# Input projection and causal pooling made one stage, with a late normalisation and the trunk stored in two halves

## What is computed

```python
h  = RMSNorm(x);  z = h @ w_in           # columns: q 512 | k/v cmp 256 | slc 256 | win 256 | gates 24 | u 512
# rope on the first 16 dims of each q and k head; sigmoid on the gates
# pooling, 4 groups of 128 channels of u, windows w = 2, 4, 8, 16:
win_sum = cs[:, t + 1, c0:c1] - cs[:, lo, c0:c1]
d = (win_sum / cnt - u32[:, T - n_out:, c0:c1]).astype(u_ext.dtype)
outs.append(d @ w_pool[g])
return jnp.concatenate(outs, axis=-1) * pool_scale
```

## Time and profile before

| | us |
|---|---|
| three runs, median (lowest to highest) | 3171.54 (3168.58 to 3177.47) |
| the profiled execution, its own time | 3173.93 |
| its span, first to last instruction | 3172.3 |
| PE busy in the span | 2825.5 (89%) |
| DVE busy | 1457.5 (46%) |
| ACT busy | 904.5 (29%) |
| POOL (GpSimd) busy | 338.6 (11%) |
| mean granted TensorE clock | 0.944 of full |

### The profile page before, as it was taken

How to read it: one execution, slowest core, us unless ns; L and a number is a source line. 1 busy time by engine, 2 the same in 40 slices (tenths; PEclk the granted TensorE clock), 3 DMA queues, 4 the chain that set the end, 5 groups by cost and what they waited for, 6 DMA issues and landing times. The chain is left out here.

```text
span 3172.3 us, 46324 instructions
## 1 busy us (share of the span) xinstructions
PE 2825.5 (89%) x17798; PEld 2592.6 (82%) x17798; DVE 1457.5 (46%) x2742; ACT 904.5 (29%) x1536; POOL 338.6 (11%) x342
## 2 busy tenths in 40 slices
PE   4999989999999998788478888677799999999997
PEld 4888879999999997788366666233789999999996
DVE  4444447445444444301437677221345444444545
ACT  4655642111111111211236556233141111111102
POOL 3444420000000000100012131211000000000000
PEclk9999999999999999899559989789899999999999
DMA  4213133112111101101200010663321111111101
GB/s 163 103 68 113 57 103 110 51 40 63 43 40 40 40 27 73 34 30 50 76 23 32 30 51 31 211 191 108 108 67 52 55 40 40 40 53 40 45 8 55
DMA packets 171244, 206.30 MB, mean 65 GB/s; under 512 B 11879, under 2 KB 155176, under 8 KB 168367
## 3 DMA queue, kind: packets, MB, share of 16 engines
q1 hardware_dynamic: 164311, 154.27, 15.9%
q0 software_dynamic: 6816, 50.49, 4.4%
HBM read 190.89 MB, written 18.01 MB: 66 GB/s over the span
## 5 line engine op out<-in xcount | busy, mean ns | idle before, releaser
L407 ACT ACTIVATE f_act_gate<-f_act_gate 128x352 f32<-128x352 f32 x132 | 65.8, 498 | 1186.1 <-DVE f_act_gate L464 1186.0
L501 DVE SCALAR_TENSOR_TENSOR trunk<-f_down,trunk 128x352 f32<-128x352 f32 x528 | 275.9, 524 | 207.7 <-PE f_down L104 207.7
L102 PE MATMUL f_up<-f_h_hi,f_gu_hi 128*128 128x352 f32 x1056 | 344.9, 327 | 0.0
L102 PE MATMUL f_gate<-f_h_hi,f_gu_hi 128*128 128x352 f32 x1056 | 344.6, 326 | 0.0
L104 PE MATMUL f_up<-f_h_hi,f_gu_lo 128*128 128x352 f32 x1056 | 343.2, 325 | 0.0
L104 PE MATMUL f_gate<-f_h_hi,f_gu_lo 128*128 128x352 f32 x1056 | 343.0, 325 | 0.0
L102 PE MATMUL f_down<-f_a_hi,f_wd_hi 128*128 128x352 f32 x1056 | 341.0, 323 | 0.0
L103 PE MATMUL f_gate<-f_h_lo,f_gu_hi 128*128 128x352 f32 x1056 | 340.9, 323 | 0.0
L103 PE MATMUL f_up<-f_h_lo,f_gu_hi 128*128 128x352 f32 x1056 | 340.6, 323 | 0.0
L103 PE MATMUL f_down<-f_a_lo,f_wd_hi 128*128 128x352 f32 x1056 | 338.8, 321 | 0.0
L104 PE MATMUL f_down<-f_a_hi,f_wd_lo 128*128 128x352 f32 x1056 | 338.4, 320 | 0.0
(11 more groups left out here) (338 smaller groups left out, 5594.7 us busy)
## 6 DMA issues: line engine op xcount, KB each, us to landing
as_pages<-in_cache_kv_slc_dram SPq DMA_DIRECT2D x192, 128.0 KB, 2.3
f_gu_raw<-in_w_ffn_gate_dram SPq DMA_DIRECT2D x44, 512.0 KB, 4.1
f_gu_raw<-in_w_ffn_up_dram SPq DMA_DIRECT2D x44, 512.0 KB, 5.4
f_wd_raw<-in_w_ffn_down_dram SPq DMA_DIRECT2D x22, 1024.0 KB, 5.0
at_spread<-saved_rows SPq DMA_DIRECT2D x16, 768.0 KB, 3.9
as_pages<-in_cache_kv_slc_dram POOLq DMA_DIRECT2D x64, 128.0 KB, 3.2
in_w_raw<-in_w_in_dram SPq DMA_DIRECT2D x4, 1304.0 KB, 6.1
x_saved<-trunk SPq DMA_DIRECT2D x1, 4224.0 KB, 16.2
```

Source lines behind the costliest of these rows:

```text
L102: pe.matmul(out, w_hi, x_hi, start=first, stop=False)
L407: act.activation(act_gate[:, b, :], act_gate[:, b, :], ACT.Silu).then_inc(silu_done, 1)
L501: dve.scalar_tensor_tensor(xT[:, m, chunk(c)], down_bank[n % 4][:, 0:CH], 0.5, xT[:, m, chunk(c)], ALU.mult, ALU.add).then_inc(down_free, 1)
```

## The change

`stage_constants` for `cos`, `sin` and `inv_count`, `stage_in_project` and `stage_pool` become one stage, `stage_project`. The constants' and the pooling inputs' loads go to GpSimd's queue, and so do all stores of results. The norm is `LateNorm`, whose temporaries lie in parts of z; the division by the root mean square is done as the results leave PSUM: for u by DVE (`take_u`, times `inv`), for z by ACT with a scale per token, for which PE turns `inv` into columns (9 products of one column).

The order of the products is u first (2 groups of 256 columns), then z in 5 groups: 256, 256, 280, 256 and 256 columns, 45 units of 24 products. The last token tile has 32 rows and isn't padded. There are three places for split weights (`own`, in z's last columns, in the trunk's first half), so that a group's split is made while the group before is multiplied. Pooling runs on DVE beside z's products, with its temporaries in the trunk's first half, and PE's maps are put behind four z units (`maps_behind`). The trunk's store, which must land before its bytes are reused, is issued in two halves behind the second load of weights. Rotations follow each group on DVE.

```diff
-def stage_in_project(nc, mem, K, xT, gain, w_in, z, z_sample, uT, outs):
-
-
-    ZG = 4
-    ZN = OFF_POOL // ZG
-    UG, UN = 2, POOL_WIDTH // 2
-    ONE = 1
+def stage_project(nc, mem, K, trunk, trunk_weights, gain, w_in, z, z_weights, z_sample, uT, outs, constants, state_pool, w_pool, pool_scale,
+                  out_prompt, out_sample):
+
+    GROUPS = ([("u", OFF_POOL + n, POOL_WIDTH // 2) for n in (0, POOL_WIDTH // 2)]
+              + [("z", OFF_CMP, KV_WIDTH), ("z", OFF_SLC, KV_WIDTH), ("z", OFF_WIN, OFF_POOL - OFF_WIN),
+                 ("z", 0, NSA_WIDTH // 2), ("z", NSA_WIDTH // 2, NSA_WIDTH // 2)])
+    WIDEST = max(n for _, _, n in GROUPS)
+    UNITS = [(i, m, c) for i in range(2) for m in range(2) for c in range(CHUNKS)]
+    U = len(UNITS)
+    UNITS += [(i, t, None) for i in range(2, len(GROUPS)) for t in range(TT)]
+    at = {u: n for n, u in enumerate(UNITS)}
+    last_of = [max(n for n, u in enumerate(UNITS) if u[0] == i) for i in range(len(GROUPS))]
+    ROWS = POOL_STATE + N_SAMPLE
+    EXT = POOL_STATE + DEC_SEQ
+    NS = DEC_BATCH * POOL_STATE
+
+    maps_behind = {(2, 6): 0, (2, 8): 1, (3, 3): 2, (3, 8): 3}
...
+        norm = LateNorm(mem, scope, None, K, "in", (z[:, 0:KT, OFF_CMP:OFF_CMP + CH], z[:, 0, 864:864 + CH],
...
+        flat = trunk[:, 0:4, :].rearrange("p k t -> p (k t)")
+        own = [mem.sb(scope, "in_w_" + part, [P, KT, WIDEST], F32R)[:] for part in ("hi", "lo")]
+        in_z = [z_weights[:, 0:KT, n:n + NSA_WIDTH // 2] for n in (0, NSA_WIDTH // 2)]
+        flat_weights = trunk_weights[:, 0:4, :].rearrange("p k t -> p (k t)")
+        in_trunk = [flat_weights[:, n:n + 2048].rearrange("p (k n) -> p k n", k=KT) for n in (0, 2048)]
+        sets = [own, in_z, own, in_z, own, in_trunk, own]
+        rot = [uT[:, i, 0:TT * 32].rearrange("p (t h d) -> p t h d", t=TT, h=4) for i in range(4)]
...
+        prompt = [flat[:, (POOL_STATE + SEQ) * i:(POOL_STATE + SEQ) * (i + 1)] for i in range(3)]
+        diff = flat[:, (POOL_STATE + SEQ) * 3:(POOL_STATE + SEQ) * 3 + T]
...
+            @block.sync
+            def _(sp):
+                def load(i):
+                    _, start, n = GROUPS[i]
+                    if i:
...
+                norm.load(sp, gain)
+                load(0)
+                load(1)
+                for half in range(2):
+                    part = slice(half * KT // 2, (half + 1) * KT // 2)
+                    sp.dma_start(outs["x"][:, part, :], trunk[:, part, :]).then_inc(x_out, 16)
+                for i in range(2, len(GROUPS)):
+                    load(i)
...
-                norm.gpsimd(pool, h_hi, h_lo)
...
-                load(0, 0, ZN)
-                sp.dma_start(outs["x"], xT[:]).then_inc(out_sem, 16)
-                with sp.Fori(1, ZG) as i:
-                    load(i, ZN * i, ZN)
-                for i in range(UG):
-                    load(ZG + i, OFF_POOL + UN * i, UN)
...
+                pool.dma_start(state[0:NS, :], state_pool.rearrange("b s n -> (b s) n")).then_inc(landed, 16)
+                pool.dma_start(w_sb[:], w_pool.rearrange("g p n -> p g n")).then_inc(landed, 16)
+                pool.dma_start(scale[:], pool_scale).then_inc(landed, 16)
+                for target, source in constants:
+                    pool.dma_start(target, source).then_inc(constants_landed, 16)
+                pool.wait_ge(rows_taken, 1)
...
+                for n, (key, off) in enumerate((("cmp", OFF_CMP), ("slc", OFF_SLC), ("win", OFF_WIN))):
+                    pool.wait_ge(rotated, n + 1)
+                    pool.wait_ge(z_taken, TT * (n + 1))
...
+                pool.wait_ge(gated, 1)
+                pool.dma_start(outs["gates"], z[0:N_SAMPLE, TT - 1, OFF_GATE:OFF_POOL]).then_inc(out_sem, 16)
+                pool.wait_ge(rotated, len(ROPES))
+                pool.dma_start(z_sample[:], z[0:N_SAMPLE, TT - 1, :]).then_inc(out_sem, 16)
...
+                def high(i):
+                    n = GROUPS[i][2]
                     act.wait_ge(w_landed, 16 * i + 16)
...
+                    if i >= 2 and sets[i] is not in_trunk:
+                        act.wait_ge(done, last_of[i - 2] + 1)
+                    if sets[i] is in_trunk:
+                        act.wait_ge(map_done, 4 * CHUNKS)
...
+                norm.square(act, trunk, 0)
+                norm.high(act, trunk, h_hi, 0)
+                norm.square(act, trunk, 1)
+                high(0)
+                norm.root(act, 0)
+                norm.high(act, trunk, h_hi, 1)
+                norm.square(act, trunk, 2)
+                norm.high(act, trunk, h_hi, 2)
+                norm.root(act, 1)
+                norm.root(act, 2)
+                high(1)
+                high(2)
+                act.wait_ge(turned, 1)
+                act.activation(state[0:ROWS, :], row_bank[0:ROWS, :], ACT.Copy).then_inc(rows_taken, 1)
                 act.wait_ge(padded, 1)
...
+                act.wait_ge(inv_col_ready, 1)
+                act.wait_ge(x_out, 32)
+                act.wait_ge(landed, 48)
+                for i in range(2, len(GROUPS)):
+                    _, start, w = GROUPS[i]
...
+                        if t == (0 if i != 4 else 2) and i + 1 < len(GROUPS):
+                            high(i + 1)
+                        n = at[(i, t, None)]
+                        act.wait_ge(done, n + 1)
+                        act.activation(z[0:rows_of(t), t, start:start + w], banks[n % 4][0:rows_of(t), 0:w], ACT.Copy,
+                                       scale=inv_col[0:rows_of(t), t:t + 1]).then_inc(z_taken, 1)
+                        if (i, t) in maps_behind:
+                            take_map(maps_behind[(i, t)])
+                    if start == OFF_WIN:
+                        act.wait_ge(z_taken, TT * (i - 1))
+                        act.activation(z[:, :, OFF_GATE:OFF_POOL], z[:, :, OFF_GATE:OFF_POOL],
+                                       ACT.Sigmoid).then_inc(gated, 1)
...
+                norm.low(dve, trunk, h_hi, h_lo, 0)
+                norm.mean_square(dve, sum_bank, 0)
+                low(0)
+                norm.low(dve, trunk, h_hi, h_lo, 1)
+                norm.invert(dve, 0)
+                norm.mean_square(dve, sum_bank, 1)
+                norm.low(dve, trunk, h_hi, h_lo, 2)
+                take_u(0, 0, 0)
+                norm.invert(dve, 1)
+                norm.mean_square(dve, sum_bank, 2)
+                take_u(0, 0, 1)
+                norm.invert(dve, 2)
+                dve.engine_nop().then_inc(inv_ready, 1)
+                take_u(0, 0, 2)
+                low(1)
+                for c in range(CHUNKS):
+                    take_u(0, 1, c)
+                dve.wait_ge(inv_turned, 1)
+                dve.tensor_copy(inv_col[:, 0:TT - 1], row_bank[:, 0:TT - 1])
+                dve.tensor_copy(inv_col[0:N_SAMPLE, TT - 1:TT], row_bank[0:N_SAMPLE, TT - 1:TT]).then_inc(inv_col_ready, 1)
+                take_u(1, 0, 0)
+                low(2)
+                for m, c in ((0, 1), (0, 2), (1, 0), (1, 1), (1, 2)):
+                    take_u(1, m, c)
+                low(3)
+                dve.wait_ge(constants_landed, 16 * len(constants))
+                dve.wait_ge(turned, 1)
+                dve.wait_ge(x_out, 32)
+                dve.wait_ge(u_taken, U)
+                for g in range(3):
+                    pool_group(g)
+                low(4)
+                pool_group(3)
+                rope(0)
+                low(5)
+                rope(1)
+                rope(2)
+                low(6)
+                rope(3)
+                rope(4)
...
-                pe.sem_inc(z_done, ONE)
-                for c in range(CHUNKS):
-                    norm.tensor(pe, sum_bank, c)
...
-                with pe.Fori(0, ZG) as i:
-                    pe.wait_ge(w_split, i + 1 + ONE)
-                    for t in range(TT):
-                        norm.wait_ready(pe, -(-min((t + 1) * P, T) // CH))
-
-                        pe.wait_ge(z_taken, TT * i + max(0, t - 3) + ONE)
-                        last = t == TT - 1
-                        tokens = slice(T - P, T) if last else slice(t * P, (t + 1) * P)
...
+                def u_unit(i, m, c, first=False):
+                    n = at[(i, m, c)]
+                    hi, lo = sets[i]
+                    room(n)
+                    if not first:
+                        pe.wait_ge(norm.lo_done, KT * (c + 1))
+                    if m == 0 and c == 0:
+                        pe.wait_ge(w_split, i + 1)
...
+                def z_unit(i, t):
+                    n = at[(i, t, None)]
+                    hi, lo = sets[i]
+                    w = GROUPS[i][2]
+                    room(n)
+                    if t == 0:
+                        pe.wait_ge(w_split, i + 1)
+                    rows, tokens = rows_of(t), slice(t * P, t * P + rows_of(t))
...
+                def map_group(g):
+                    pe.wait_ge(diff_ready, g + 1)
...
+                for i in range(2, len(GROUPS)):
```

(12 more changed lines are left out.)

339 lines of the change are left out of this document (144 added, 195 removed).

## The result

| | before | after |
|---|---|---|
| median of the runs | 3171.4 us (4 runs, 3168.6 to 3177.5) | 3092.4 us (4 runs, 3091.7 to 3096.0) |
| the profiled execution, span beside it | 3173.93, span 3172.3 | 3091.68, span 3089.9 |
| mean granted TensorE clock | 0.944 | 0.954 |

The ratio is 0.9751, with a 95% interval of 0.9734 to 0.9768: 79 us less, where 71 were forecast (3100.5, range 3079 to 3122).

What follows compares the result with a forecast made beforehand. It took PE as the bound, with waits for split weights, norm and pooling uncovered: 3173.93 less 3.2 (constants), 6.6 (norm), 47.6 (products), 18.8 (pooling), plus 5 (clock), less 2.4, gave 3100.5 us; range 3092 to 3112, 8-in-10 3079 to 3122.

Steps and rivals of the forecast that it cites:

- clock term: New stage: slow clock behind the third sum's wait and at the thin stretch of the transposes, 5 us lost.
- next unit after the square: Norm: the unit of products behind the third sum starts 28.0 us after the first square.
- four map groups: Pooling's maps on PE: 2.0 us each, 8 us in all left on PE's path.
- Constants and norm: Start of the stage: 3.2 us gained by dropping the constants stage, 6.6 us by the norm.
- wait for the third sum: Norm: PE waits some 5 us for DVE to free the bank of the third sum of squares.
- Products: u and z products: 225.5 us become 177.9, as waits for split weights and slow clock behind them go; 47.6 us gained.
- Pooling: Pooling, 38.2 us before: window sums run free on DVE beside z; 18.8 us gained.
- Tail: Behind the last z unit: ACT's copy 0.6, rotation 2.5, store 4.2 and barrier 0.7, 8.0 us in all.
- More holes than counted: Rival, 15%: dearer map groups and slow stretches at group changes add 21 us, giving 3122 us.
- Slower: Rival, 4%: z stays at half clock after the transposes, costing 103 us, giving 3203 us.
- The store gates the stage: Rival, 1%: the trunk's two store halves land later than 74 us in, so banks fill after 4 units.
- The next stage speeds up: Rival, 8%: the compress stage runs at full clock behind dense work, saving 22 us, giving 3079 us.

Runs made afterwards that it cites:

- e0: The changed kernel again, unedited, for a second profile: 3093.9 us, ratio 0.9749 to the kernel before.
- e1: The changed kernel with one pair of split-weight tiles for all groups: 3134.0 us, ratio 0.9872 to the kernel before.
- e2: The changed kernel with all four map groups ahead of the first z unit: 3115.0 us, ratio 0.9821 to the kernel before.
- e6: The changed kernel with the store of z_sample on SP's queue instead of GpSimd's: 3094.5 us, ratio 0.9749 to the kernel before.
- e3: The changed kernel with the third sum of squares behind the second unit of products, not the first: 3087.7 us, ratio 0.9731 to the kernel before.
- e4: The changed kernel with the trunk's store in one piece ahead of the second weight load: 3096.9 us, ratio 0.9763 to the kernel before.
- e9: The changed kernel with unread multiplications (10 tail, 72 and 12 compress stage) and DVE's second-weight low part later: 3078.3 us, ratio 0.9698 to the kernel before.
- e10: The changed kernel with third sum later, z_sample store on SP, last rotation split, unread multiplications and DVE's new compress order: 3072.2 us, ratio 0.9673.
- e8: The changed kernel with unread multiplications: 10 in the tail, 72 ahead of the compress stage's first wait, 16 behind its transposes: 3079.7 us median.

## Why the prediction was right

The mechanism held, but for the second place of the clock term, and the time came 8 us below the forecast, at the very bottom of its own range of 3092 to 3112. (The sum as written, 3171.54 less 71.2, gives 3100.3; the recorded 3100.5 is a slip of 0.2.) The stage from its first load: 226.5 forecast, 223.2 measured. By the steps:

| step | forecast, us | measured, us |
|---|---|---|
| square behind SP's first load | 0.1 | 0.0 (1245.64 both) |
| first product after the square | 14.4 | 13.2 (15.1 in e0) |
| next unit after the square | 28.0 | 29.3 |
| 11 units of u, with the turned `inv` | 43.2 | 46.7 |
| transposes | 2.4 | 1.7 |
| z, 36 narrow and 9 wide units | 131.8 | 129.6 |
| four map groups | 8.0 | 8.4 |
| tail | 8.0 | 7.4 |
| clock, kept apart | 5.0 | in the rows above |

*Constants and norm.* The constants came as forecast. The first product came 1.2 us early, and that is luck: the first sum took 5.00 us in this profile, where it took 7.34 in the feed-forward stage that the forecast was read from (the row below) and 8.02 in e0. The wait for the third sum was 5.0 us, as said; that sum took 7.4 us and not 5.0, which is the clock term in its place.

```profile
461.24 7.34 PE L287 MATMUL f_down<-f_sq,ones 128*128 128x352 f32 x16 [5.46 <-ACT f_sq L268]
```

*Products.* z's units were 2.83 us apart (36 of them) and 3.08 (9), 0.118 and 0.128 us for a product where I had taken 0.12 and 0.13 from the earlier trace rows: 2.2 us less by rounding. PE is busy 137.9 of 138.1 us. e1 is the proof of the step: with one pair of weights 27.0 us of waits and 12.9 besides come back, 39.9, of the 47.6 that the prediction gave to the products (27.3 of it waits). What the other 7.7 hang on, the new order and the new widths among others, no run separates. The 2.3 us of clock that it put behind a wait of 5 were 2.1.

*Pooling.* The maps cost 2.09 us each (a z unit with a map behind it took 4.92 where others took 2.83), the 2.0 of the forecast. That the window sums are free under z, and 24.9 us without it, is e2: 21.3 us more, since three of the maps then hide behind DVE.

*Tail.* 7.4 us for 8.0. The store and the barrier took 4.16 together, from the store's issue to the next stage's first load, where 4.2 and 0.7 had been put down: the transfer lands in 2.4 us, less than the 3 to 8 that I had allowed the store, and the signals and the barrier take the other 1.8. The Trainium skill, page DMA: Bandwidth & Descriptors, section on the SWDGE path, has a fit that gives 2.4 us for these 163 KB, as the prediction cited it, and this trace's 2.4 agrees; it was the better of the two figures. The Trainium skill's warning against GpSimd's queue, on the same page in the section SWDGE vs HWDGE vs iDMA, showed no effect here that the time could tell (e6).

*Clock.* The 5.0 us were the right size at one right place and one wrong one. The third sum lost 2.4 us; the products right behind it were already 0.16 us apart. The transposes, which were to be the second place, ran at clock 1.00. The second place was the turned `inv`: its 18 instructions of one column took 2.09 us where I had 1, and behind them the clock was at 0.68 for the next 5 us although PE's row shows no idle time in them:

```profile
1294.58 2.09 PE L1636 MATMUL pl_row_bank<-ones,in_inv 1*128 1x1 f32 x18
```

```profile
1295.00:1300.00 5.00, 5.00 (x28) 4.97 (x28) 0.43 (x3) 1.66 (x1) 0.00 (x0) 0.68 0.01 3
```

The unit behind it ended 7.61 us after the one before, where two others were 3.86 apart: 3.75 us for a step that the forecast had at 1. The 2.09 are the step's own, the same in every run; the other 1.66 came in some profiles and not in others, with either length of the third sum ahead (e3), and why stays open. The two losses of clock together are 4.1 us, for the 5.0 put down.

*What is left.* 226.5 less 223.2 is 3.3 us of the 8. The others are outside the stage, in untouched code, where e0 and the other profiles show a scatter of 3.6 and 5.5 us in two stretches. The kernel before stood near its upper end. I call this scatter; no experiment looked for a cause of it.

*The rivals.* More holes than counted (15%): no; the maps left no hole and no change of group has one. Slower (4%): no; in e2 z ran at the full level behind a much longer thin stretch, and in e1 its products brought the level back behind each wait. (By its own rows, 0.21 against 0.12 and 0.13 us for a product, it would have cost 99 us and not 103.) The store gates the stage: no, e4. The next stage speeds up (8%): not in this change, though e9 shows the 19 us are there to be had. The reason that the prediction gave against it, that PE has nothing to do in the tail and in the 21.5 us up to the next stage's first product, fits e9, where products fill those gaps; e9 also has products right ahead of the stage's own, so which of the two counted isn't separated. The one that it gave beside it, from the earlier trace rows, that these products at half clock don't raise it, is also true, but only half of it: at the full level the same products keep it (e9).

## What to carry to other kernels

A wait of TensorE costs its length and, here, about 2 us more behind it, so the waits to take away first are the many short ones; a second set of operands, even one that borrows memory not yet in use, is worth both. Work of another engine that needs little of TensorE was free here under a dense stretch but for TensorE's own part of it, if its few multiplications are put in where its results are long ready. And look at the stage behind: a level lost in the gap between stages can stay lost through a whole dense stage, and an order of instructions that was harmless at half clock turns into the next hole at full clock.

## What the runs showed of the hardware that was not expected

- The compress stage's 192 products, with PE busy 45.0 of 45.5 us, ran at the half level (1.2 GHz) to the end when they began there, and at the full level (2.4 GHz) to the end in e9, busy 24.1 of 24.6 us. The unread float32 passes, of as many columns, went from 0.50 to 1.00 within 3 to 5 us (e9, e10), and z's products of 280 columns within the 5 us behind a wait (e1). The Trainium skill, page TensorE: Matmul & The Clock Gate, Part 1, holds that activity releases the throttle: in e1, e9 and e10 the trace agrees, in the compress stage of the changed kernel it doesn't. What sets those products apart from the unread ones is open.
- A hole of 1.4 us was followed by the half level for all of the 33.6 us that were left (e8's slowest execution; two others of the same kernel took 20 us less), one of 0.46 us by nothing in e9 and by 20 us of half level in e10. The same 2.88 us between two stages left the first sum at 5.00 us in some executions and at 8.02 in others. So a short hole is a risk more than a price, and where the products behind it don't raise the clock it can cost some ten times its length (33.6 us of products at half the pace behind 1.4 us).
- Eighteen instructions of one column, with no idle time of PE in the records, were followed by a clock of 0.67 to 0.70 over 5 us in six profiles and by 1.00 in five, the changed kernel being among both. One profile of a kernel can't show that an edit took such a loss away.
